# Attention: one VectorE operation for each block of scores, and another order of the stage's first steps

## What is computed

```python
qkv = h @ w_qkv                       # 16 query heads, 4 key/value heads, 64 wide
q, k = apply_rope(q), apply_rope(k)
s = (q @ k^T) / sqrt(64)              # 128-row blocks of queries; keys: this block and the one before
s = where(0 <= dist < 128, s, finfo(float32).min)
p = softmax(concat([s, sink]))[..., :-1]      # sink: one learned number for each head
o = (p @ v) @ w_o
```

## Time and profile before

| | |
|---|---|
| time, median of 3 runs | 924.43 us (924.32 to 925.01) |
| the profiled execution | 925.67 us |
| its span | 923.4 us |
| attention stage in it, from its first projection to the last output matmul | some 646 to 736 us |
| TensorE busy | 912.8 us, 99% |
| VectorE busy | 742.8 us, 80% |
| ScalarE busy | 444.4 us, 48% |
| GpSimd busy | 27.9 us, 3% |
| granted TensorE clock, mean | 0.998 of full speed |
| HBM read | 167.31 MB, 182 GB/s over the span |

### The profile page before, as it was taken

How to read it: one execution, slowest core, us unless ns; L and a number is a source line. 1 busy time by engine, 2 the same in 40 slices (tenths; PEclk the granted TensorE clock), 3 DMA queues, 4 the chain that set the end, 5 groups by cost and what they waited for, 6 DMA issues and landing times.

```text
span 923.4 us, 12980 instructions
## 1 busy us (share of the span) xinstructions
PE 912.8 (99%) x4172; PEld 755.2 (82%) x4172; DVE 742.8 (80%) x1319; ACT 444.4 (48%) x621; POOL 27.9 (3%) x53
## 2 busy tenths in 40 slices
PE   8999999999999999999999999999999999999997
PEld 6888888888888888888888888888788888888885
DVE  6988888768987988888889878887866689788884
ACT  6453544455434534435355353444666473544433
POOL 1000000000000000000010000000411000000000
PEclk9999999999999999999999999999999999999999
DMA  8766574446743674655457656475520188565631
GB/s 295 254 196 214 164 223 158 160 146 252 263 163 110 212 230 152 220 188 184 148 169 247 209 171 221 154 221 187 179 94 19 49 283 264 162 217 168 204 115 46
DMA packets 122101, 168.83 MB, mean 183 GB/s; under 512 B 8588, under 2 KB 98772, under 8 KB 122068
## 3 DMA queue, kind: packets, MB, share of 16 engines
q1 hardware_dynamic: 121792, 168.09, 55.6%
q10 hardware_dynamic: 276, 0.30, 0.1%
HBM read 167.31 MB, written 1.05 MB: 182 GB/s over the span
## 4 chain that ended last, share of the span: by engine, by line
PE 96%; DMA 1%; DVE 1%; ACT 1%; issue 0%; POOL 0%; SPq 0%; POOLq 0%; ACTq 0%
PE acc L1219 31%; PE proj L1203 20%; PE proj L1204 20%; PE proj L1205 20%; PE tp L1256 1%; PE proj L1280 1%; DMA raw_in<-in_w_ff_in 1%; DMA raw_in<-in_attn_w_qkv 1%; PE acc L1412 1%; PE acc L1438 1%; PE proj L1412 1%; PE tp L1438 1%; PE tp L1269 1%; DVE in_lo L773 0%; ACT scratch L646 0%
## 5 line engine op out<-in xcount | busy, mean ns | idle before, releaser
L1203 PE MATMUL proj<-in_hi,xT_hi 128*128 128x512 f32 x840 | 329.3, 392 | 0.2 <-issue 0.2
L1205 PE MATMUL proj<-in_hi,xT_lo 128*128 128x512 f32 x840 | 327.0, 389 | 0.0
L1204 PE MATMUL proj<-in_lo,xT_hi 128*128 128x512 f32 x840 | 326.8, 389 | 0.0
L773 DVE TENSOR_TENSOR in_lo<-raw_in,in_hi 128x1024 fp32r<-128x1024 f32 x208 | 246.2, 1224 | 38.1 <-ACT in_hi L460 37.9
L460 ACT ACTIVATE in_hi<-raw_in 128x1024 fp32r<-128x1024 f32 x208 | 209.1, 1051 | 12.6 <-DMA raw_in<-in_w_ff_in 3.9
L845 DVE STREAM_TRANSPOSE scratch<-gated 32x128 f32<-32x128 f32 x640 | 193.4, 302 | 8.3
L1203 PEld LDWEIGHTS proj<-in_hi,xT_hi 128*128 128x128 f32 x840 | 157.7, 188 | 33.4 <-issue 0.8
L1205 PEld LDWEIGHTS proj<-in_hi,xT_lo 128*128 128x128 f32 x840 | 157.7, 188 | 32.9
L1204 PEld LDWEIGHTS proj<-in_lo,xT_hi 128*128 128x128 f32 x840 | 157.7, 188 | 32.5 <-issue 0.2
L509 ACT ACTIVATE hT_hi<-scratch 128x512 fp32r<-128x512 f32 x40 | 25.4, 634 | 258.8 <-DVE scratch L845 258.8
L780 DVE TENSOR_TENSOR out_lo<-raw_out,out_hi 128x1024 fp32r<-128x1024 f32 x96 | 113.2, 1220 | 2.9 <-ACT out_hi L468 2.7
(11 more groups left out here) (126 smaller groups left out, 463.9 us busy)
## 6 DMA issues: line engine op xcount, KB each, us to landing
raw_in<-in_w_ff_in SPq DMA_DIRECT2D x344, 256.0 KB, 6.3
raw_out<-in_w_ff_out SPq DMA_DIRECT2D x88, 512.0 KB, 5.2
raw_in<-in_conv_w_in SPq DMA_DIRECT2D x24, 512.0 KB
raw_in<-in_attn_w_qkv SPq DMA_DIRECT2D x12, 512.0 KB
raw_out<-in_conv_w_out SPq DMA_DIRECT2D x8, 512.0 KB, 5.5
raw_out<-in_attn_w_o SPq DMA_DIRECT2D x8, 512.0 KB, 3.8
scratch<-in_w_ff_in SPq DMA_DIRECT2D x8, 256.0 KB
x<-in_x SPq DMA_DIRECT2D x2, 512.0 KB, 5.4
```

The source lines that it names most:

```text
L773: dve.tensor_tensor(in_lo[:, slot, 2 * q:2 * q + 2, :], raw[:, 2 * q:2 * q + 2, :], in_hi[:, slot, 2 * q:2 * q + 2, :].bitcast(F32), ALU.s ...
L1203: pe.matmul(proj[t][:, :], x_hi, in_hi[:, slot, k, :], start=(k == 0), stop=False)
L1204: pe.matmul(proj[t][:, :], x_hi, in_lo[:, slot, k, :], start=False, stop=False)
L1205: last = pe.matmul(proj[t][:, :], x_lo, in_hi[:, slot, k, :], start=False, stop=(k == KD - 1))
```

## The change

`mask_max` has one `tensor_tensor_reduce` for each head in place of the three instructions for a group. It writes (score + band) · (-1/8), so `pair` holds negated scores, and its second output is the minimum of these and of the negated sink, which is `neg_max`. The exponential reads with scale -1. The semaphores between the three steps go; `masked` now says that the whole of it is done. On TensorE, the second tile's projection is no longer cut before its end, two slices of the next projection go ahead of the scores, and `transpose_qk(3)` comes one slice earlier in that projection. On ScalarE, the split of the output unit's first half goes behind `qk_out(2)` and the table load, `exps(0)` goes ahead of `qk_out(3)`, and the second half's split behind `probs_out(0)`. On VectorE, the first half's split goes behind the masks of groups 0 and 1, and the second half's behind the mask of group 2. `row_max` is not written any more.

```diff
--- before.py
+++ after.py
@@ -278,8 +278,6 @@
         qkT_ready = sem("qkT_ready")
         scores_done = sem("scores_done")
         masked = sem("masked")
-        max_step = sem("max_step")
-        neg_max_ready = sem("neg_max_ready")
         exp_done = sem("exp_done")
         sink_arg_ready = sem("sink_arg_ready")
         sink_exp_done = sem("sink_exp_done")
@@ -649,11 +647,11 @@
 
                     def exps(g):
                         t, heads = attention_group(g)
-                        act.wait_ge(neg_max_ready, g + 1)
+                        act.wait_ge(masked, g + 1)
                         keys = W // len(heads)
                         for n, h in enumerate(heads):
                             part = pair[:, g % 2, n * keys:(n + 1) * keys]
-                            act.activation(part, part, ACT.Exp, bias=neg_max[:, t, h:h + 1],
+                            act.activation(part, part, ACT.Exp, scale=-1.0, bias=neg_max[:, t, h:h + 1],
                                            accum_out=prob_sum[:, t, h:h + 1]).then_inc(exp_done, 1)
 
                     def sink_exps(b):
@@ -684,16 +682,16 @@
                     v_rows(1)
                     split_in(u + 2, (u + 2) % 2, range(PIECES))
                     qk_out(0)
-                    split_out(o + 1, (o + 1) % 2, (0,))
                     qk_out(1)
                     qk_out(2)
                     act.activation(warm[:, :], minus_half[:, :], ACT.Exp)
-                    split_out(o + 1, (o + 1) % 2, (1,))
+                    split_out(o + 1, (o + 1) % 2, (0,))
+                    exps(0)
                     qk_out(3)
-                    exps(0)
                     exps(1)
                     sink_exps(0)
                     probs_out(0)
+                    split_out(o + 1, (o + 1) % 2, (1,))
                     exps(2)
                     probs_out(1)
                     next_piece(0)
@@ -1062,23 +1060,19 @@
                         dve.wait_ge(scores_done, g + 1)
                         if g >= 2:
                             dve.wait_ge(probT_ps, g - 1)
-                        buf = pair[:, g % 2, :].rearrange("p (h n) -> p h n", n=keys)
-                        dve.scalar_tensor_tensor(out=buf, in0=scores[g // 6][g % 2][:, :].rearrange("p (h n) -> p h n", n=keys),
-                                                 scalar=1.0 / math.sqrt(HD),
-                                                 in1=band[:, 2 * P - keys:2 * P].unsqueeze(1).to_broadcast([P, len(heads), keys]),
-                                                 op0=ALU.mult, op1=ALU.add).then_inc(masked, 1)
-                        dve.wait_ge(masked, g + 1)
-                        hs = slice(heads[0], heads[-1] + 1, 2)
-                        dve.tensor_reduce(row_max[:, t, hs], buf, AX.X, ALU.max, negate=True).then_inc(max_step, 1)
-                        dve.wait_ge(max_step, g + 1)
-                        dve.tensor_tensor(neg_max[:, t, hs], row_max[:, t, hs], neg_sink[:, hs],
-                                          ALU.min).then_inc(neg_max_ready, 1)
+                        for n, h in enumerate(heads):
+                            part = slice(n * keys, (n + 1) * keys)
+                            last = dve.tensor_tensor_reduce(out=pair[:, g % 2, part], in0=scores[g // 6][g % 2][:, part],
+                                                            in1=band[:, 2 * P - keys:2 * P], scale=-1.0 / math.sqrt(HD),
+                                                            scalar=neg_sink[:, h:h + 1], op0=ALU.add, op1=ALU.min,
+                                                            accum_out=neg_max[:, t, h:h + 1])
+                        last.then_inc(masked, 1)
 
                     def sink_args(b):
 
                         half, t = divmod(b, 2)
                         hs = slice(8 * half, 8 * half + 8)
-                        dve.wait_ge(neg_max_ready, BATCH_LAST[b] + 1)
+                        dve.wait_ge(masked, BATCH_LAST[b] + 1)
                         dve.tensor_tensor(sink_arg[:, t, hs], neg_max[:, t, hs], neg_sink[:, hs],
                                           ALU.subtract).then_inc(sink_arg_ready, 1)
 
@@ -1453,14 +1447,14 @@
                     transpose_qk(0)
                     queries(1, 1, range(0, HALF))
                     transpose_qk(1)
-                    queries(1, 1, range(HALF, HALF + 2))
+                    queries(1, 1, range(HALF, KD))
                     transpose_qk(2)
-                    queries(1, 1, range(HALF + 2, KD))
+                    queries(2, 0, range(0, 2))
                     score(0)
                     score(1)
-                    queries(2, 0, range(0, HALF + 1))
+                    queries(2, 0, range(2, HALF))
                     transpose_qk(3)
-                    queries(2, 0, range(HALF + 1, KD))
+                    queries(2, 0, range(HALF, KD))
 
                     through = (2, 4, 5, 7, 8)
                     for g in range(6):
```

## The result

| | before | after |
|---|---|---|
| time, median of 19 runs | 924.49 us (923.54 to 925.3) | 922.76 us (922.2 to 923.7) |
| the profiled execution | 925.67 us | 922.41 us |
| its span | 923.4 us | 920.1 us |
| shared start to first matmul of the next stage | 67.75 us (667.87 to 735.62) | 65.95 us (666.47 to 732.42) |

What follows compares the result with a forecast made beforehand. TensorE bounds the kernel, busy 912.8 of 923.4 us. The front's 1.6 us and group 6's 0.1 make 1.7 us, taking the median from 924.43 to 922.7 us, range 921.9 to 924.1.

Steps and rivals of the forecast that it cites:

- the front: TensorE from 667.87 to transpose_probs(0): pauses before query transposes, scores and first transposed probabilities go, 1.6 us gained.
- group 6: The only mask group without slack: a shorter mask starts its exponentials earlier and brings TensorE 0.1 us.
- the restart: TensorE's transpose blocks after a standstill take longer: 0.06 us at transpose_qk(2), some 0.05 at transpose_probs(0), which goes.
- The covers: Inputs of TensorE's moved blocks are ready in time: GpSimd and qk_out(2) 0.6 us ahead, group 0's exponentials 1.3 or more.
- The mask: New VectorE operation: 0.36 us for 128 columns; four heads take 1.45 us instead of 1.52, two heads 1.00.
- My estimate from the page's figures: Four-head mask group on VectorE by 120 cycles plus one per element at 0.96 GHz: 1.03 us, total the same to 0.1.
- The dear mask: Rival at group 6: mask becomes the bound, pauses from 1.6 us for four heads, 925.0 at the upper end; chance 0.07.
- The piece that I added for group 7: In the mask rival, group 7, a second four-head group right behind group 6 on VectorE, adds some 0.3 us.
- My upper end of 3.5 us: Upper bound for a four-head mask group on VectorE, from 0.88 us an operation; first pause then 1.9 us.
- The front does not do what it says: Rival at TensorE's front: next waits stand close behind, a pause of up to 0.8 us stays, 923.5 to 924.4; chance 0.07.
- the 0.2% line: Whole kernel: differences under 0.2%, 1.85 us, cannot be told from none; faster than 922.58 us had chance 0.36.

Runs made afterwards that it cites:

- e1: The kernel before with TensorE's new order alone, mask and the ScalarE and VectorE orders as before: 923.10 us, ratio 0.9982 to the kernel before.
- e3: The kernel before with the new orders of TensorE, ScalarE and VectorE, mask still in three instructions: 922.92 us, ratio 0.9982 to the kernel before.
- e4: The kernel before with the new mask operation and negated exponentials, all engines in the old order: 924.35 us, ratio 0.9998 to the kernel before.
- e6: The changed kernel with the four mask operations of group 6 done twice: 923.41 us, ratio 0.9987 to the kernel before.
- e7: The changed kernel with every group's mask operations done twice: 923.45 us, ratio 0.9989 to the kernel before.
- e5: The changed kernel without the two slices of the next projection ahead of the scores, which follow behind them: 923.56 us, ratio 0.9992 to the kernel before.
- e9: The kernel before with TensorE's new order alone and one more 128x1024 copy on ScalarE: 923.84 us, ratio 0.9999 to the kernel before.

## Why the prediction was right, and where it was only lucky

*The time.* 922.7 was forecast and 922.76 measured, a gain of 1.7 us of which 1.6 was to be the front and 0.1 group 6. In the profiles the stretch lost 1.80: transpose_probs(0) came 1.57 us earlier (9.82 against 11.39, forecast 9.83), the restart 0.05, group 6 0.13. Both terms held, and e1, e3 and e4 separate them: orders 1.63, mask 0.12 to 0.17. The closeness of the first is in part two slips that cancel. The terms from 667.87 on add up to 677.77 and not to 677.7, so the front would have been worth 1.49 us and 0.05 for the restart. And the scores, taken at 1.81 us from a row behind a pause, took 1.70 (669.91 to 671.61).

*The covers.* transpose_qk(2), the scores and transpose_probs(0) follow at 0.23 us. GpSimd ended 0.4 us ahead of the transposes (667.69, 668.08; forecast 0.6), qk_out(2) 0.6 ahead of the scores (669.31, 669.91; forecast 0.6), and the exponentials of group 0 ended 2.4 us ahead of their transposes (673.86, 676.29; forecast 1.3 or more, though its own instants, 676.2 and 677.7, are 1.5 apart). No load was late for the output split.

*The mask.* Its size was the term that I had least right. I took 0.36 us for each of four operations and 1.45 for the group; the rows show 0.35 long but 0.27 apart, 1.09 for the group, and 0.81 instead of 1.00 for two heads. The error is that I added 0.02 for the second output and nothing for the overlap of neighbours, which is 0.08 for each. It changed nothing in the sum, since beyond 0.12 us TensorE had no more to gain there. The new operations do count as two instructions each, as the Trainium skill says in "VectorE: DVE Perf Modes", section "Two Vector instructions with no wait between them"; the second is 0.08 us and hides under the next. But eight instructions took 1.09 us where three took 1.52, so the advice of its "Rules for kernel authors" to minimise the count of operations would have chosen wrongly here. The likely reason is that two of the three went over all 512 columns, 0.72 us each, and the eight go over them once; cutting the one pass in four is dear in itself (1.09 against 0.72), as the advice has it. The three also stood behind semaphores: 0.72 apart at 0.69 long, where two operations of that length without a wait between them start 0.61 apart (670.99 and 671.60 in the kernel before). Neither the pass nor the semaphore was tried alone. My estimate from the page's figures, 1.03, was nearer than my own.

*The rivals.* The dear mask fell by its price, and e6 and e7 confirm its place: a pause at group 6 and nowhere else. The piece that I added for group 7 was not reached at 2.18 us a group: doubling all groups added 0.06 us to doubling group 6. My upper end of 3.5 us was not tried. "The front does not do what it says" fell for the changed kernel, but its mechanism is real: e5 shows the next wait 0.9 us behind, and e9 shows it when ScalarE is late.

*What failed.* "The scores start 0.54 us after the last projection matmul: 0.31 us. What they wait for is ScalarE's copy" stopped one link too early. I took 0.31 for a property of the kernel; it is the landing time of one weight quarter plus 5.84 us, and the pause was 0.31 in the profile that I had, and 0.80 (669.26 to 670.29) in the next one of the same kernel. With that one the same sum would have given 2.2 us and a time of 922.2: still in the range, but on the other side of the 0.2% line, where I had put a chance of 0.36. The measured ratio (1.9 us) lies between the two. So whether the forecast fell inside 0.2% or outside was a matter of which profile I held, and the interval of the ratio reaches over both sides.

## What to carry to other kernels

When one engine is the bound and its order is written by hand, read its pauses from distances of starts, and lay the new order out instant by instant; a block moved away from its late input must find enough work behind it too, or the pause only moves one block on. Follow each pause back until the chain reaches a load or the bounding engine itself: if it ends at a load, its length is a sample, and a second profile of the same kernel is worth more than another decimal. A cheaper operation on an engine that is not the bound is worth only the slack that it lacks, here 0.13 us, where VectorE is busy for 6.3 us less (742.8 and 736.5).

## What the runs showed of the hardware

- A fused operation with a minimum as second output, 128x128 from PSUM with a per-row scalar, takes 0.35 us, 128x256 takes 0.48; neighbours without a wait start 0.27 and 0.40 apart, and the read of the accumulator (0.08) starts together with the next operation. No run has the operation without that read.
- Where VectorE and GpSimd both work from SBUF to SBUF, the one that began first kept its time and the other took longer. In the changed kernel the split of 1.22 us began at 665.18 and kept it, and GpSimd's half sum, begun at 665.34, took 1.65 us where it takes 0.73 without a split beside it. At 678.55 GpSimd was first: its half sum kept 0.74, and the output split, begun at 678.60, took 1.77. At 693.44 and 693.54 VectorE was first again (1.23 and 1.72).

```profile
665.18 1.22 DVE L771 TENSOR_TENSOR in_lo<-raw_in,in_hi 128x1024 fp32r<-128x1024 f32 x1
...
673.38 1.22 DVE L778 TENSOR_TENSOR out_lo<-raw_out,out_hi 128x1024 fp32r<-128x1024 f32 x1
...
678.60 1.77 DVE L778 TENSOR_TENSOR out_lo<-raw_out,out_hi 128x1024 fp32r<-128x1024 f32 x1
```

```profile
665.34 1.65 POOL L415 TENSOR_TENSOR scratch<-gated 128x256 f32<-128x256 f32 x1 [3.68 <-DVE gated L1051]
...
669.65 0.73 POOL L415 TENSOR_TENSOR scratch<-gated 128x256 f32<-128x256 f32 x1 [1.96 <-DVE gated L1051]
...
678.55 0.74 POOL L416 TENSOR_TENSOR scratch<-gated 128x256 f32<-128x256 f32 x1
```

The masks, with one input in PSUM, keep their 0.48 beside the same GpSimd work (677.79 and 678.20, GpSimd from 677.85).

- The landing of one 512 KB quarter, relative to TensorE's order, moved by 1.25 us over the profiles of this study (the split that waits for it began 1.89 to 3.14 us ahead of the shared start), though the program ahead of it was the same and the row of four loads that it belongs to was issued within 0.04 us of the same instant.
